# A list of one-hot rows made by TensorE and ScalarE instead of GpSimd, in the pair-grid stage of a two-block transformer kernel

## The reference, cut to what matters

```python
top, pos = lax.top_k(cand, PEER_TOPK)
idx = jnp.take_along_axis(cidx, pos, axis=-1)      # i1 * 128 + i2
gate = jax.nn.softmax(top, axis=-1)
...
u = expert_down[ib]
act = jax.nn.gelu(jnp.einsum('bld,blhkd->blhk', hb, u), approximate=False)
coef = (gb * act.astype(F32)).astype(hb.dtype)
vv = expert_up[ib]
return jnp.einsum('blhk,blhkd->bld', coef, vv)
```

## Time and profile before

| | us |
|---|---|
| three runs | 4469.19, 4469.32, 4475.35 |
| median of the runs | 4469.32 |
| the profiled execution | 4463.62 |
| its span (first to last instruction) | 4461.8 |
| of it `peer_grid`, first VectorE instruction to end of the last | 3935.72 to 4090.35 |

### The profile page before, as it was taken

How to read it: one execution, slowest core, us unless ns; L and a number is a source line. 1 busy time by engine, 2 the same in 40 slices (tenths; PEclk the granted TensorE clock), 3 DMA queues, 4 the chain that set the end, 5 groups by cost and what they waited for, 6 DMA issues and landing times. The chain is left out here.

```text
span 4461.8 us, 55085 instructions
## 1 busy us (share of the span) xinstructions
PE 3830.0 (86%) x21625; PEld 3205.0 (72%) x21625; DVE 2292.1 (51%) x2676; ACT 1899.1 (43%) x2085; POOL 194.2 (4%) x284
## 2 busy tenths in 40 slices
PE   6899878987948778999999997598668699977999
PEld 1792866987938556777777775598347699976887
DVE  0332623443345226888888773333431388645665
ACT  0333151433342416666666662333321344454554
POOL 0000000000000000000000000000000000076000
PEclk8999878998959779999999998799569899977999
DMA  7456003534500117999999994144002265511665
GB/s 243 160 182 226 5 9 110 183 132 151 185 9 1 50 45 256 336 347 342 343 345 346 345 344 169 57 170 160 0 6 102 79 183 183 180 57 34 193 193 165
DMA packets 305410, 738.76 MB, mean 166 GB/s; under 512 B 13465, under 2 KB 13920, under 8 KB 305248
## 3 DMA queue, kind: packets, MB, share of 16 engines
q1 hardware_dynamic: 305248, 736.59, 47.6%
HBM read 735.50 MB, written 1.05 MB: 165 GB/s over the span
## 5 line engine op out<-in xcount | busy, mean ns | idle before, releaser
L1767 DVE TENSOR_TENSOR weight_ring_low<-weight_ring,weights_high 128x2048 fp32r<-128x2048 f32 x336 | 761.5, 2308 | 245.9 <-ACT weights_high L1711 245.7
L1711 ACT ACTIVATE weights_high<-weight_ring 128x2048 fp32r<-128x2048 f32 x336 | 624.9, 1908 | 275.4 <-DMA weight_ring<-in_moe_w 274.2
L304 PE MATMUL psum_all<-h_high_projections,high_projections 128*128 128x256 f32 x1536 | 434.8, 283 | 50.0 <-DVE weight_ring_low L340 50.0
L304 PE MATMUL psum_all<-h_low_projections,high_projections 128*128 128x256 f32 x1536 | 434.1, 283 | 0.0
L304 PE MATMUL psum_all<-h_high_projections,weight_ring_low 128*128 128x256 f32 x1536 | 431.1, 281 | 0.0
L1655 PE MATMUL psum_all<-weights_high,expert_in_turn_high 128*128 128x512 f32 x896 | 361.0, 403 | 58.5 <-DVE weight_ring_low L1767 58.5
L340 DVE TENSOR_TENSOR weight_ring_low<-weight_ring,high_projections 128x2048 fp32r<-128x2048 f32 x96 | 215.4, 2289 | 302.2 <-ACT high_projections L326 302.2
L1655 PE MATMUL psum_all<-weights_high,expert_in_turn_low 128*128 128x512 f32 x896 | 356.5, 398 | 0.0
L1655 PE MATMUL psum_all<-weight_ring_low,expert_in_turn_high 128*128 128x512 f32 x896 | 353.3, 394 | 0.0
L304 PEld LDWEIGHTS psum_all<-h_high_projections,high_projections 128*128 128x128 f32 x1536 | 291.3, 190 | 51.2 <-issue 51.2
L2594 PE MATMUL psum_all<-peer_h_high,expert_rows_high 128*128 128x256 f32 x1024 | 290.8, 284 | 5.0 <-DVE expert_rows_low L2644 5.0
(11 more groups left out here) (559 smaller groups left out, 7912.5 us busy)
## 6 DMA issues: line engine op xcount, KB each, us to landing
weight_ring<-in_moe_w SPq DMA_DIRECT2D x168, 2048.0 KB, 7.8
weight_ring<-in_w_in SPq DMA_DIRECT2D x48, 2048.0 KB, 8.5
expert_rows<-in_peer_down SPq DMA_DIRECT2D x128, 512.0 KB, 3.6
expert_rows<-in_peer_up SPq DMA_DIRECT2D x128, 512.0 KB, 3.6
weight_ring<-in_ada_w SPq DMA_DIRECT2D x24, 2048.0 KB, 8.0
weight_ring<-in_ffn_w SPq DMA_DIRECT2D x21, 2048.0 KB, 7.7
weight_ring<-in_w_out SPq DMA_DIRECT2D x6, 2048.0 KB, 8.0
weight_ring<-in_w_up_dn SPq DMA_DIRECT2D x4, 2048.0 KB, 7.9
```

What stands on the lines that cost most here:

```text
L304: mm = pe.matmul(half(k.ps, 4 * (g % R) + j), w[:, c, j * P:(j + 1) * P], x[:, c], start=(c == 0 and n == 0), stop=(c == KC - 1 and n == 2))
L1711: act.activation(high[:, q, h * HALF:(h + 1) * HALF], k.ring[:, (g0 + q) % R, h * HALF:(h + 1) * HALF], ACT.Copy).then_inc(high_made[q], 1)
L1767: dve.tensor_tensor(k.low[:, (g0 + q) % R, part], k.ring[:, (g0 + q) % R, part], high[:, q, part].bitcast(F32), ALU.subtract).then_inc(low ...
```

## The change

`peer_second`, the plain rows, is now made for four tokens at a time by TensorE and ScalarE. TensorE writes `column - i2` for the 4 x 128 columns of a block into PSUM bank `4 + n % 4` by two matmuls: the identity times the column of `-i2` repeated 128 times, and a row of ones times the row 0, 1, ..., 127 repeated four times (one row deep). Both are in float32r (one record each) with 512 columns. ScalarE squares the block (L2744 of the kernel after) into `peer_apart` and takes Relu of 1 minus that into `peer_second` (L2752). VectorE makes all four gated rows of each block. GpSimd makes nothing. For float32r operands there are three new tables (`ident`, `ones`, `iota`), copied once by VectorE in `peer_scores`, and `peer_lists` shrinks from five lists to two, beside `-i2` in its own tile.

```diff
@@ peer_scores, VectorE
             dve.tensor_tensor(m.h_low[:], k.h, m.h_high[:].bitcast(F32), ALU.subtract).then_inc(h_split, 1)
+            for dst, src in ((m.ident, k.ident), (m.ones, k.ones), (m.iota, k.iota)):
+                dve.tensor_copy(dst[:], src).then_inc(h_split, 1)
@@ peer_values, ScalarE
                     act.activation(m.lists[:, 0], half(k.ps, 8), ACT.Copy).then_inc(moved, 1)
-                    act.activation(m.lists[:, 1], half(k.ps, 9), ACT.Copy).then_inc(moved, 1)
-                    act.activation(m.lists[:, 2], half(k.ps, 10), ACT.Copy).then_inc(moved, 1)
-                    act.activation(m.lists[:, 3], half(k.ps, 8), ACT.Copy, scale=-1.0).then_inc(moved, 1)
-                    act.activation(m.lists[:, 4], half(k.ps, 10), ACT.Copy, scale=-1.0).then_inc(moved, 1)
+                    act.activation(m.lists[:, 1], half(k.ps, 10), ACT.Copy).then_inc(moved, 1)
+                    act.activation(m.i2_minus[:], half(k.ps, 9), ACT.Copy, scale=-1.0).then_inc(moved, 1)
@@ peer_grid, GpSimd
             st.clear_last(pool)
-            for n in range(N):
-                if n >= 4:
-                    pool.wait_ge(multiplied, n - 3)
-                for q in range(QUAD):
-                    t = n * QUAD + q
-                    pool.tensor_scalar(m.second[:, n % 4, q], k.iota, i2[:, t:t + 1], None, ALU.is_equal).then_inc(made_c, 1)
@@ peer_grid, ScalarE
+            def square(n):
+                act.wait_ge(apart, n + 1)
+                if n >= 4:
+                    act.wait_ge(made_second, n - 3)
+                act.activation(m.apart[:, n % 4], k.ps[:, 4 + n % 4, :], ACT.Square).then_inc(squared, 1)
+            square(0)
             for n in range(N):
+                if n + 1 < N:
+                    square(n + 1)
                 if n >= 4:
                     act.wait_ge(multiplied, n - 3)
-                for q in range(2):
-                    t = n * QUAD + q
-                    act.activation(m.apart[:, (2 * n + q) % 8], k.iota, ACT.Square, bias=i1_minus[:, t:t + 1]).then_inc(squared, 1)
-                for q in range(2):
-                    t = n * QUAD + q
-                    act.wait_ge(squared, 2 * n + q + 1)
-                    act.activation(m.first[:, n % 4, q], m.apart[:, (2 * n + q) % 8], ACT.Relu, bias=g[:, t:t + 1],
-                                   scale=g_minus[:, t:t + 1]).then_inc(made_a, 1)
+                act.wait_ge(squared, n + 1)
+                act.activation(m.second[:, n % 4].rearrange("p q j -> p (q j)"), m.apart[:, n % 4], ACT.Relu, bias=1.0,
+                               scale=-1.0).then_inc(made_second, 1)
@@ peer_grid, VectorE, first(n)
-                for q in range(2, QUAD):
+                for q in range(QUAD):
@@ peer_grid, TensorE
+            def distance(n):
+                if n >= 4:
+                    pe.wait_ge(squared, n - 3)
+                out = k.ps[:, 4 + n % 4, :]
+                pe.matmul(out, m.ident[:], col_bc(m.i2_minus[:, n * QUAD:(n + 1) * QUAD], NK), start=True, stop=False)
+                pe.matmul(out, m.ones[0:1], row_bc(m.iota[0:1], QUAD), start=False, stop=True).then_inc(apart, 1)
+            distance(0)
+            distance(1)
+            distance(2)
             for n in range(N):
-                pe.wait_ge(made_a, 2 * n + 2)
-                pe.wait_ge(made_b, 2 * n + 2)
-                pe.wait_ge(made_c, QUAD * n + QUAD)
+                if n + 3 < N:
+                    distance(n + 3)
+                pe.wait_ge(made_first, QUAD * n + QUAD)
+                pe.wait_ge(made_second, n + 1)
```

More of the change, by code:

```diff
@@ L2467, in __init__ @@
         self.grid = k.sb("pair_grid", [P, NK, T], ctx=ctx)
-        self.lists = k.sb("peer_lists", [P, 5, T], ctx=ctx)
+        self.lists = k.sb("peer_lists", [P, 2, T], ctx=ctx)
+        self.i2_minus = k.sb("peer_second_list", [P, T], F32R, ctx=ctx)
+        self.ident, self.ones, self.iota = (k.sb(f"peer_{n}", [P, P], F32R, ctx=ctx) for n in ("ident", "ones", "iota"))
         def units(name, first, n, dt, shape=None):
@@ L2478, in __init__ @@
         self.second = units("peer_second", PEER_RAW + 2, 2, F32, [P, 4, QUAD, NK])
-        self.apart = units("peer_apart", PEER_RAW + 4, 1, F32, [P, 8, NK])
+        self.apart = units("peer_apart", PEER_RAW + 4, 2, F32, [P, 4, QUAD * NK])
         self.coef_high = units("peer_coef_high", PEER_RAW + PEER_HIGH, 1, F32R, [P, 4, T])
@@ L2725, in peer_grid @@
     N = T // QUAD
-    i1, i2, g, i1_minus, g_minus = (m.lists[:, n] for n in range(5))
+    i1, g = m.lists[:, 0], m.lists[:, 1]
     with k.stage("peer_grid") as st:
         block = st.block
-        made_a, made_b, made_c, squared, multiplied, weighed = st.signals(6)
+        apart, squared, made_first, made_second, multiplied, weighed = st.signals(6)
         @block.gpsimd
@@ L2759, in first @@
                     dve.wait_ge(multiplied, n - 3)
-                for q in range(2, QUAD):
+                for q in range(QUAD):
                     t = n * QUAD + q
-                    dve.tensor_scalar(m.first[:, n % 4, q], k.iota, i1[:, t:t + 1], g[:, t:t + 1], ALU.is_equal, ALU.mult).then_inc(made_b, 1)
+                    dve.tensor_scalar(m.first[:, n % 4, q], k.iota, i1[:, t:t + 1], g[:, t:t + 1], ALU.is_equal, ALU.mult).then_inc(made_first, 1)
             first(0)
```

## The result

The changed kernel takes 4512.2 us (median of four runs, 4506.1 to 4520.1) against 4472.3 for the kernel before on the same chip: a ratio of 1.0088, with a 95% interval of 1.0068 to 1.0109. That is 40 us slower, where 47 faster was forecast. The profiled execution took 4506.1 us with a span of 4504.0.

What follows compares the result with a forecast made beforehand. GpSimd bounds the stage before the change, VectorE after it at 1.69 us a block. The stage gives 46.1 us and the head of peer_mix 1.5, 47.6 less than the 4469.3 median: 4421.7 us, range 4412 to 4450.

Steps and rivals of the forecast that it cites:

- Which clock: In the changed stage TensorE, busy 1.45 of every 1.69 us (86%), runs at the full clock.
- TensorE's term: Per four-token block: new matmuls plus products take 1.45 to 1.58 us at full clock, 2.6 to 2.9 at half.
- The half-clock rival: Stage entered at half clock stays there; TensorE bounds, 2.6 to 2.9 us a block, 4485 to 4504; chance 0.04.
- VectorE's term: Per block: 0.61 us behind a start of L2770 plus four row makers at 0.27, 1.69 us, bounding the stage.
- the rival of slow pairs: VectorE's rows stay as slow as beside GpSimd: 2.05 us a block, 24 us less, 4445 us; chance 0.09.
- ScalarE's term: Per block: square and Relu 0.59 us each, about 1.2 (high end 1.6), under 1.69, so never last.
- The stage: From VectorE's first row at 3935.72 to the last L2770: ends 4044.2 against 4090.35, 46.1 us less, near 109 us.
- The head of peer_mix: Its eight one-row matmuls, 7.2 us at half clock, may partly run at full: between 0 and 3.6, 1.5 us less.

Runs made afterwards that it cites:

- experiment 5: Changed kernel with the second new matmul 128 rows deep and sixteen one-row matmuls put in behind the third pair of distances: 4425.4 us, ratio 0.9905.
- experiment 7: Changed kernel with the second new matmul 64 rows deep and sixteen one-row matmuls ahead of the stage's first block: 4435.4 us, ratio 0.9914.
- experiment 8: Changed kernel with the second new matmul 8 rows deep and sixteen one-row matmuls ahead of the stage's first block: 4510.0 us, ratio 1.0094.
- experiment 2: Changed kernel with sixteen extra one-row matmuls behind the third pair of distances, into a bank overwritten later: 4516.5 us, ratio 1.0114.
- experiment 1: Changed kernel with sixteen extra 128-row matmuls behind the third pair of distances, into a bank overwritten later: 4429.0 us, ratio 0.992.
- experiment 3: Changed kernel with the second new matmul 128 rows deep (table of 1/128 times all rows of the column numbers): 4419.1 us, ratio 0.9896.
- experiment 6: Changed kernel with the second new matmul 64 rows deep (table of 1/64 times 64 rows of the column numbers): 4425.7 us, ratio 0.991.
- experiment 4: Kernel before, with VectorE making all four gated rows of a block, ScalarE none, GpSimd still the plain rows: 4468.5 us, ratio 1.0012.
- experiment 9: Changed kernel with the second new matmul 128 rows deep and peer_mix's zero matmuls full-row float32r from a table made in peer_scores: 4407.1 us, ratio 0.9869.

## Why the prediction was wrong

**The step that failed is "Which clock".** "I take the full clock for the stage" stands there, from a busy share of 86%. The trace shows 0.50 with a TensorE that is busy without a gap. The step's second sentence, that back-to-back work raises the clock "as in the stretch from which the clock rose", was carried from blocks of four full-row products to a block with a one-row matmul in it. The warning was in view: 24 us of busy TensorE at 0.50 with 16-row matmuls among them. Experiments 5, 7 and 8 settle it: from the same half-clock state the clock comes back in the second block with 128 rows and with 64, and not in 190 us of blocks with 8 rows, nor in the blocks with one row of experiment 2. In the changed kernel itself it came back only where the one-row matmuls ended, in the last three blocks. The busy share was the wrong measure.

**The other half of the cause is the head.** The prediction let the stage keep the clock that it comes with. Blocks with one-row matmuls held the full clock in experiment 1 (1.00 from 3941.5 to 4052.0), but the head of the changed kernel loses it within 3.5 us, and then they don't win it back. No wait between matmuls stands at the fall, and there is no coming and going: 1.00 up to 3933.30, 0.75 from there to 3934.24 with TensorE busy 0.94 of 0.94 us, then 0.50 up to 4123.40 with 189.16 of 189.16 us busy. What tips the head is its second matmul's depth too: the same four pairs lost the clock with one row (changed kernel, and behind three pairs in experiment 1) and kept it with 128 rows (experiment 3, 1.00 from 3939.6 to 3941.7) and with 64 (experiment 6, at the same pace, 1.00 from 3941.0 to 3944.4). Why one-row matmuls lost the clock in pairs by themselves here and held it in experiment 1's blocks with products is open.

**TensorE's term was mis-sized at both clocks.** The pair of new matmuls was put at 0.45 us at the full clock and 0.85 at the half; it measured 0.81 (0.39 and 0.42, experiment 1) and 1.43 (0.71 and 0.72, the changed kernel), since two loads per block are uncovered. With the products, 0.91 and 1.73 to the next block, that makes 1.72 a block in place of 1.45, and 3.16 in place of 2.6 to 2.9. At full clock this would have cost little: TensorE in place of VectorE as the bound, 1.72 against 1.63 a block, 6 us over 64. With full rows the term is right within 0.1 us: experiment 5's first block that is wholly at the full clock has 0.54 from L2778 to the products (3956.40 to 3956.94) and 1.34 in all (to 3957.74), where 1.45 stood. The rows taken for the pair were both full-row ones, and the difference in row count was not priced.

**The half-clock rival named the right bound and the right clock**, with 0.04 for a chance, but not the way there: its condition was a stage entered at the half, and this one was entered at 1.00 and lost it inside. It said 4485 to 4504, and 16 to 35 us more; with 3.15 a block its own sum gives 64 x 3.15 + 4 = 206 against 154.6, 51 more. Measured were 45: the last three blocks have no new matmuls ahead of them, which that sum didn't allow for.

**VectorE's term held.** Four rows 1.11 us where 4 x 0.27 stood, 0.60 from L2770 to the next row, 1.63 a block where 1.69 stood. Without GpSimd's row makers the rows of this stage keep the pace of the first six, and the rival of slow pairs falls. Beside GpSimd four rows took mostly 1.16 to 1.36 us (experiment 4); by what it slows them no run here shows.

**ScalarE's term held.** 597 ns for the square where 0.59 us stood, 622 for Relu, 1.2 together; it waits 123.6 us in the changed kernel.

**The stage.** 109 us was forecast, and 104.7 came in experiment 3 (3939.7 to 4044.4), with the first L2770 3.6 us behind VectorE's first row (3.5 forecast). In the changed kernel it came 5.6 behind, at the half clock. Put on the scale of the forecast, experiment 3 is 0.9896 x 4469.3 = 4422.8 beside the 4422 that was predicted. That it comes so close is partly luck: the stage gave 49.9 us where 46.1 were forecast, and what lies behind the stage took 2.2 longer where 1.5 less was forecast (373.7 against 371.4), so that two errors of 3.8 and 3.7 cancel.

**The head of peer_mix** was to gain 1.5. It gained nothing: the eight one-row records take 7.19 as before, behind the same 2.80 of waiting. The reason given for the term, a stage left at the full clock, doesn't help: experiment 3 left it at 1.00, and the eight records ran at 0.50 in 7.19 us again. To the first expert product it is 1.3 longer, in the changed kernel and in experiment 3, because the 32 records behind them (adding the residual) take 6.6 us in both where they took 5.3; why is open.

## What to carry over

A busy TensorE is not a fast one (50 of 50 us busy at 0.50 in the changed kernel and at 1.00 in experiment 1): before work is moved to it, read the granted clock in stretches with matmuls of the same row count, and distrust busy stretches at the half. Give a broadcast matmul all rows (a table of 1/128 in place of one row of ones) rather than one: here this was worth 1.9%, 86 us, by the ratios of the changed kernel and of experiment 3. And where the forecast hangs on a level that lasted at either of two values here (1.00 in experiment 1, 0.50 in experiment 2), the chance of the other is not 0.04 just because the busy share speaks for one.

## What the runs showed of the hardware

- The same stage code ran at either clock with TensorE busy 50.00 of 50.00 us (3990 to 4040): at 1.00 behind sixteen matmuls of 128 rows (experiment 1, 4429.0 us), at 0.50 behind sixteen of one row (experiment 2, 4516.5 us).
- At the head of the stage, pairs of 512-column matmuls with a second one of one row took the clock from 1.00 to 0.50 with no gap between them (changed kernel, 3930.72 to 3934.24). The same pairs kept 1.00 with 128 rows (experiment 3, 3939.6 to 3941.7) and, at the pace of the changed kernel, with 64 (experiment 6, 3941.0 to 3944.4).
- From the half clock, a block with a 128-row or a 64-row second matmul got back to the full clock in its second block (1.00 from 3956.40 in experiment 5, from 3954.85 in experiment 7). With 8 rows the clock was 0.50 over 190.3 us (experiment 8, 3949.7 to 4140.0), with one row over 153 us (experiment 2, 3947 to 4100), at the same pace of issue for 64 and 8 rows.
- A weight load next to a matmul of another row count was not covered here. At the full clock the starts inside the blocks are 0.39 to 0.43 us apart with one row (experiment 1) and with 64 (experiment 6), in place of 0.21 to 0.30 between full-row ones (experiment 3, 3939.68 to 3943.56). At the half they are 0.70 to 0.73 apart with 1, 8 and 64 rows (changed kernel, experiments 8 and 7). L2779's load starts together with its matmul and takes 0.18 us at the full clock (experiment 1, 4002.38) and 0.28 at the half (changed kernel, 4012.35).
- Eight one-row records behind a pause of 2.80 us ran at 0.50, whether the stage before them ended at 1.00 (experiment 3) or at 0.93 (changed kernel), and took 7.19 us in both. Four full-row ones behind a pause of 1.05 us ran at 1.00 and took 1.11 us (experiment 9).
